# Cross-attention query panels without pieces between them, the norm root ahead of a cast, and the decode softmax ahead of heads 1 to 3

## What is computed

```
def cross_attn(h, mk, mv, w_q, w_o):
    q = (h @ w_q).reshape(B, T, X_HEADS, X_HEAD_DIM)           # 4 heads of 128
    s = jnp.einsum('bthd,bmhd->bhtm', q, mk) * (X_HEAD_DIM ** -0.5)
    p = jax.nn.softmax(s, axis=-1)
    o = jnp.einsum('bhtm,bmhd->bthd', p, mv).reshape(B, T, X_DIM)
    return o @ w_o
xp = xp + cross_attn(rmsnorm(xp, g_cross), mk, mv, w_xq, w_xo)                    # 256 tokens, one memory of 256
xs = xs + cross_attn(rmsnorm(xs, g_cross), cache_mem_k, cache_mem_v, w_xq, w_xo)  # 8 tokens, a memory of 256 each
```

## Time and profile before

| what | value |
|---|---|
| median of 3 runs | 1651.37 us (1646.44 to 1657.36) |
| profiled execution | 1649.72 us, its span 1648.0 us |
| TensorE busy | 1521.5 us, 92% of the span |
| VectorE busy | 1031.0 us, 63% |
| ScalarE busy | 612.7 us, 37% |
| mean granted TensorE clock | 0.966 of full speed |
| query stage | 736.3 us (first xq pass) to 822.9 us (first xo pass) |

### The profile page before, as it was taken

The page is one execution under the profiler, slowest core; times in us unless marked ns, Lnnn a source line. Parts: engine busy times, 40 slices in busy tenths (PEclk is TensorE's granted clock), DMA queues, the critical chain, the costliest instruction groups (busy, mean ns, idle before and its releaser), DMA issues.

```text
span 1648.0 us, 32704 instructions
## 1 busy us (share of the span) xinstructions
PE 1521.5 (92%) x12249; PEld 1408.8 (85%) x12249; DVE 1031.0 (63%) x3226; ACT 612.7 (37%) x721; POOL 235.1 (14%) x331
## 2 busy tenths in 40 slices
PE   4999987799898899998789999999999999999997
PEld 4999864577776677998589999999999999999996
DVE  4579899998976876665365555554444555554444
ACT  3342232232233453443354333333333333333443
POOL 3011222222222222330140000000000000000221
PEclk9999989999998999997799999999999999999998
DMA  8558999999998799552335555544555555553553
GB/s 319 179 180 303 405 361 413 407 378 373 373 383 312 265 401 398 177 180 77 128 125 175 184 181 178 178 154 158 177 184 198 184 184 184 181 178 125 187 179 123
DMA packets 78980, 388.42 MB, mean 236 GB/s; under 512 B 9097, under 2 KB 9873, under 8 KB 56865
## 3 DMA queue, kind: packets, MB, share of 16 engines
q1 hardware_dynamic: 35424, 230.90, 39.1%
q0 software_dynamic: 39376, 143.15, 23.1%
q10 hardware_dynamic: 4080, 13.12, 2.0%
HBM read 377.03 MB, written 10.10 MB: 235 GB/s over the span
## 4 chain that ended last, share of the span: by engine, by line
PE 74%; DVE 14%; DMA 5%; ACT 4%; issue 3%; ACTq 0%; DVEq 0%; SPq 0%; POOLq 0%; POOL 0%
PE bank L1541 22%; PE bank L1542 21%; PE bank L1543 21%; DVE page L1082 4%; DVE wlo L1026 3%; DMA page<-kc_dram 2%; PE bank L1698 2%; ACT whi L601 1%; ACT whi L564 1%; DMA raw<-p_out_dram 1%; DVE wlo L991 1%; PE bank L1894 1%; DMA raw<-p_in_dram 1%; DMA page<-vc_dram 1%; DVE rstd L1017 1%
## 5 line engine op out<-in xcount | busy, mean ns | idle before, releaser
L1541 PE MATMUL bank<-hh,whi 128*128 128x264 f32 (+1 forms) x2368 | 696.3, 294 | 36.9 <-DVE wlo L1026 23.9
L1542 PE MATMUL bank<-hl,whi 128*128 128x264 f32 (+1 forms) x2368 | 678.5, 287 | 0.0
L1543 PE MATMUL bank<-hh,wlo 128*128 128x264 f32 (+1 forms) x2368 | 677.9, 286 | 0.0
L991 DVE TENSOR_TENSOR wlo<-raw,whi 128x2048 fp32r<-128x2048 f32 (+1 forms) x174 | 357.9, 2057 | 276.1 <-ACT whi L564 276.1
L1541 PEld LDWEIGHTS bank<-hh,whi 128*128 128x128 f32 x2368 | 454.5, 192 | 73.9 <-issue 41.7
L564 ACT ACTIVATE whi<-raw 128x2048 fp32r<-128x2048 f32 (+1 forms) x174 | 299.3, 1720 | 552.9 <-PE bank L1543 545.4
L1542 PEld LDWEIGHTS bank<-hl,whi 128*128 128x128 f32 x2368 | 454.8, 192 | 0.7 <-issue 0.2
L1543 PEld LDWEIGHTS bank<-hh,wlo 128*128 128x128 f32 x2368 | 452.2, 191 | 0.0
L1082 DVE CUSTOM_DVE_ANT_0 page<-page,qb 128x128 f32<-128x128 f32 x1024 | 226.2, 283 | 16.5 <-ACT qb L646 11.4
L1541 PE MATMUL bank<-f_hi,whi 128*128 128x264 f32 x704 | 201.9, 287 | 7.5 <-DVE f_lo L1513 7.5
L1543 PE MATMUL bank<-f_hi,wlo 128*128 128x264 f32 x704 | 201.4, 286 | 0.0
(11 more groups left out here) (296 smaller groups left out, 1434.9 us busy)
## 6 DMA issues: line engine op xcount, KB each, us to landing
raw<-p_gu_dram SPq DMA_DIRECT2D x88, 1024.0 KB, 4.9
page<-kc_dram POOLq DMA_DIRECT2D x128, 512.0 KB, 8.1
page<-vc_dram POOLq DMA_DIRECT2D x128, 512.0 KB, 8.4
raw<-p_in_dram SPq DMA_DIRECT2D x48, 1024.0 KB, 8.4
raw<-p_dn_dram SPq DMA_DIRECT2D x64, 704.0 KB, 4.1
raw<-p_out_dram SPq DMA_DIRECT2D x16, 1024.0 KB, 5.2
raw<-p_mem_dram SPq DMA_DIRECT2D x8, 1024.0 KB, 8.3
x_res<-x_fm_dram SPq DMA_DIRECT2D x8, 528.0 KB, 10.5
```

Source lines behind the costliest of these rows:

```text
L991: tt(wlo[:, (k + 2) % 4, 0:blocks * P], raw[:, (k + 2) % 4, 0:blocks * P], whi[:, k % 2, 0:blocks * P], ALU.subtract).then_inc(S("w_split" ...
L1541: mm(out, blk(whi, k % 2, b), rh, start=start, stop=False)
L1542: mm(out, blk(whi, k % 2, b), rl, start=False, stop=False)
L1543: return mm(out, blk(wlo, k, b), rh, start=False, stop=stop)
```

## The change

Nothing is added or taken away; instructions change places on three engines. On TensorE panels 0 and 1 run without any piece up to the last quarter of panel 1; a head's rows move from the first quarter of the next panel to its third, its spread from the second quarter of the next panel to the first quarter of the panel after that, and head 0's score, transposition and value product move back accordingly. On ScalarE the root stands ahead of the cast of panel 2. The decode softmax moves ahead of head 2's maximum on VectorE and ahead of head 2's exponential on ScalarE.

```
@@ -890,29 +890,29 @@
                 wait_apart(act, "a_ops", n + 1)
                 act.activation(oh[:, i:i + 1, 0:NP_], row(a_set(n)[-1][:, 0:256]), ACT.Copy).then_inc(S("a_ohi"), 1)
 
+            norm_root(2, T)
             step("xq", 0, 0, C)
-            norm_root(2, T)
             x_rows(0)
+            step("xq", 0, 1, C)
             x_stage(0)
-            step("xq", 0, 1, C)
+            x_rows(1)
             x_exp(H)
-            x_rows(1)
+            step("xq", 0, 2, C)
             x_scale(H)
-            step("xq", 0, 2, C)
-            x_pt(H)
             x_rows(2)
             step("xq", 0, 3, C)
+            x_pt(H)
+            x_rows(3)
             x_out_hi(H, 0)
-            x_rows(3)
             x_stage(1)
+            x_exp(H + 1)
             x_stage(2)
-            x_exp(H + 1)
+            x_scale(H + 1)
+            act.wait_ge(S("x_sub"), 1)
+            act.activation(x_p[:, :, :, 0:XH], x_s, ACT.Exp).then_inc(S("x_exp"), 1)
             x_exp(H + 2)
-            x_scale(H + 1)
             x_pt(H + 1)
             x_scale(H + 2)
-            act.wait_ge(S("x_sub"), 1)
-            act.activation(x_p[:, :, :, 0:XH], x_s, ACT.Exp).then_inc(S("x_exp"), 1)
             x_pt(H + 2)
             x_out_hi(H + 1, 1)
             x_take(0)
@@ -1420,14 +1420,14 @@
             x_start()
             ch.link(dve.memset(x_p, 0.0))
             step("xq", 0, 0, C, to_q)
+            step("xq", 0, 1, C, to_q)
             x_scores(0)
             x_max(H)
-            step("xq", 0, 1, C, to_q)
+            step("xq", 0, 2, C, to_q)
             x_rec(H)
             x_scores(1)
-            step("xq", 0, 2, C, to_q)
+            step("xq", 0, 3, C, to_q)
             x_scores(2)
-            step("xq", 0, 3, C, to_q)
             x_out_lo(H, 0)
             x_start()
             x_max(H + 1)
@@ -1436,18 +1436,18 @@
             bh = "p (b h) -> p b h"
             tt(x_sm[:, 0:32].rearrange(bh, b=ND), x_s[:, :, 0, :], x_s[:, :, 1, :], ALU.max).then_inc(S("x_small"), 1)
             x_rec(H + 1)
-            x_max(H + 2)
             dve.wait_ge(S("x_small_ps"), 1)
             ch.link(dve.tensor_reduce(x_sm[0:32, 64:65], bank[5][0:32, 0:P], AX.X, ALU.max))
             ts(x_sm[0:32, 96:128], ident[0:32, 0:32], x_sm[0:32, 64:65], None, ALU.mult).then_inc(S("x_small"), 1)
-            x_rec(H + 2)
             dve.wait_ge(S("x_small_ps"), 2)
             mb = bank[5][:, P:P + 32].rearrange(bh, b=ND)
             for m in range(2):
                 ins = tt(x_s[:, :, m, :], x_s[:, :, m, :], mb, ALU.subtract)
             ins.then_inc(S("x_sub"), 1)
+            x_max(H + 2)
             dve.wait_ge(S("x_exp"), 1)
             tt(x_sm[:, 32:64].rearrange(bh, b=ND), x_p[:, :, 0, 0:XH], x_p[:, :, 1, 0:XH], ALU.add).then_inc(S("x_small"), 1)
+            x_rec(H + 2)
             x_out_lo(H + 1, 1)
             x_start()
             dve.wait_ge(S("x_small_ps"), 3)
@@ -1940,20 +1940,19 @@
 
             for k in range(4):
                 x_quarter(k, 0)
+                if k >= 2:
+                    x_spread(k - 2)
+                x_quarter(k, 1)
+                if k == 2:
+                    x_head(0)
+                x_quarter(k, 2)
                 if k:
                     x_rows(k - 1)
-                x_quarter(k, 1)
-                if k:
-                    x_spread(k - 1)
-                x_quarter(k, 2)
-                if k == 1:
-                    x_head(0)
-                elif k == 2:
-                    x_turned(H)
-                elif k == 3:
-                    x_out(H)
                 x_quarter(k, 3)
+            x_turned(H)
+            x_spread(2)
             x_rows(3)
+            x_out(H)
             for k in range(2):
                 pe.wait_ge(S(f"acc{k}_free"), ACC["xq"] // 2 + 3)
             x_head(1)
@@ -1961,9 +1960,9 @@
             x_head(2)
             pe.wait_ge(S("x_small"), 1)
             pe.transpose(bank[5][0:32, 0:P], x_sm[:, 0:32], ident).then_inc(S("x_small_ps"), 1)
-            x_turned(H + 1)
             pe.wait_ge(S("x_small"), 2)
             mm(bank[5][:, P:P + 32], ones[0:32, :], x_sm[0:32, 96:128], start=True, stop=True).then_inc(S("x_small_ps"), 1)
+            x_turned(H + 1)
             x_turned(H + 2)
             x_out(H + 1)
             pe.wait_ge(S("x_small"), 3)
```

## The result

| | before | change |
|---|---|---|
| median beside each other on one chip | 1649.32 us (4 runs, 1646.44 to 1657.36) | 1633.05 us (4 runs, 1631.62 to 1637.91) |
| ratio | | 0.9902 [0.9873, 0.993] |
| profiled execution, span | 1649.72, 1648.0 us | 1634.03, 1632.3 us |
| mean granted clock | 0.966 | 0.970 |

The change is faster by 1.0%; the spans of the two profiled executions differ by 15.7 us. Of these 15.4 lie in the cross query stage: from the norm sum (L1593, which runs 0.34 us earlier than before) to the first output pass (L1541 with `oh`) the stage took 81.19 us before and 65.80 now.

A forecast was written before the change was run, and what follows sets the result against it. The stage was taken as bound by TensorE's in-order list, waits on pieces within it and the low clock. From 1649.72, -20.5 + 3.1 + 2.2 + 0.9 + 0.7 = -13.6 gives 1636.1, median-adjusted 1637.8, stated as 1637 us; range 1629 to 1645.

The forecast's parts named there:

- A: The panels, to panel 3's evacuation: 20.5 us shorter if nothing waits and the clock stays up.
- the margins of 1.6 and 0.8 us: TensorE asks for x_q[0] 1.6 us after it is ready, and for panel 2's split 0.8 us after.
- the removed wait: TensorE's 4.75 us wait for VectorE's x_q at the end of panel 0, which the change was to remove.
- The clock: Within the panels: a fall to 1.2 GHz after each of two spreads, 3.4 us each, costing +3.1 us, bounds 0 and 6.2.
- rival 1: The clock stays up in the panels and beyond: -19.1 us, 1630.6, or 1632 carried to the median; chance 0.18.
- B: End of panel 3 to the decode softmax: a chain of cast, split, scores, spread 3, scores; +2.2 us.
- C: Decode softmax to first value product, with the softmax moved ahead of head 2: +0.9 us, bounds 0 and +2.
- D: First value product to first output panel: same work, clock perhaps back later; +0.7 us, bounds 0 and 3.4.
- The case with the highest chance: Whole kernel: a time within 1% of before, neither below 1634.9 nor above 1667.9 us; chance 0.63.

The follow-up runs named there:

- wide spreads: Spreads multiply 128 zero-padded rows in place of 8: ratio 0.9872 on the change, 0.9946 on the kernel before, 0.9917 on that with the root ahead.
- VectorE's list cleared: The change with 128-row spreads, first value product ahead of head 2's transposition, output panels' splits later on VectorE: 0.9885, or 0.9876 with splits in two gaps.
- the repeat: The change itself, unaltered, timed once more beside the kernel before: ratio 0.9895.
- values first: The change with head 1's value product, the decode sums and the first value product ahead of head 2's transposition: ratio 0.9851.

## Why the prediction was right

**A.** The sum of passes, spreads, head and transpositions was right. It put the end of panel 3, at the full clock, 24.5 us behind the norm sum (2.86 to 744.55, and 21.6). In the change panel 3 ended 26.2 us behind it (767.57); without the 1.5 us of the one fall that is 24.7. VectorE was scoring head 1 and reached the evacuation 0.6 us later, at 768.16, which makes 26.81; the prediction had no such term. With wide spreads and no fall A was 25.05, and with VectorE's list cleared 23.90. No wait was left; the margins of 1.6 and 0.8 us held, the second as 1.0 (split done at 747.5, panel 2 from 748.5).

Where the 18.2 us come from the experiments tell, with 0.45 us lost for each low microsecond. Before, A without its 23.9 low microseconds would be 34.3 us (measured with one fall left: 35.12 - 1.5 = 33.6). The root ahead brings it to 30.1, the order of the panels to 25.05. So, all with wide spreads, 3.5 us are the root's (33.6 to 30.14), 5 us the order's, and 9 us (0.45 x the 20.5 low microseconds that went) the clock's; 0.4 us are assigned to none. The other runs agree: beside the repeat, the six runs of the change were on average 16.9 us shorter than the eleven of before and, by the mean granted clock of each, 19.8 us less at 1.2 GHz, which is 9 us. The prediction had the sum, but its text named the removed wait first; half of the gain was the clock.

**The clock.** The term was +3.1 us for two falls of 3.4 us; the profiled execution had one (+1.5), the repeat two. The mechanism was as read from the earlier trace rows: a fall with TensorE busy throughout, behind a spread. The rule of the Trainium skill that was weighed (TensorE: Matmul & The Clock Gate, section "HAM oscillation"), that pauses between bursts cost the clock, is borne out for the pause of 4.76 us, behind which the clock fell even with wide spreads; it does not cover the fall at 752.5, ahead of which the trace has no pause. Panels without a fall, as in rival 1, did occur: in the change with values first, whose panels are the same. How often the clock falls cannot be told from one trace, and the range had to hold both.

**B.** The chain of the prediction came out term by term: cast at 767.61, split at 769.55, scores, spread 3 at 775.32 with 3.75 us, scores, L1437 at 782.56. From the start of the cast it is 14.95 us, where 14.9 was summed. In the repeat A changed by -17.2 us, where -17.4 was forecast, and B by +2.3, where +2.2 was.

**C** was the term that was mis-sized: +0.9 forecast, -0.14 measured (0 was its lower bound). The prediction charged head 2's maximum 2 us for standing behind the decode maximum and gave only half of it back. In the trace both exchanges cancel, and with the softmax moved back C is 0.14 us longer: this part of the change is worth nothing that the runs can show.

**D** grew by 1.24 us, forecast 0.7, and by 0.05 us in the repeat: the term goes with the clock and differs from execution to execution. In the first one the first two value products and the scores of head 3 still ran at 1.2 GHz (1.08 and 0.99 us for the products, against 0.64), the clock returned some 5 us behind the first value product, and before within 1 us of it (granted clock 0.81 from 809 to 810 us, 1.00 from there).

The differences of all stretches make the forecast 2.1 us too slow in the trace. The median is 4 us under it: 1637 forecast, 1633.05 measured beside 1649.32, which is itself 2 us under the 1651.37 from which the prediction started. The case with the highest chance, a time within 1% of before, came true by very little: the ratio is 0.9902, and its interval reaches to both sides of 0.99. On which side it came to lie is luck.

## What to carry to other kernels

When a wait of one engine's list goes, sum the stage again at the full clock and price the clock apart: here half of the gain was 20 us at 1.2 GHz that went when the wait and the pieces between the passes did. A small matmul group among large passes may cost more afterwards than while it runs, so compare the clock behind it with a form that fills the array. And work that is moved into a gap has to be put there again each time something ahead of it moves.

## What the runs showed that was not expected

- A spread of 16 matmuls on 128 rows of zero-padded weights takes no longer than one on 8 rows, and the clock behaves otherwise behind it. Of the executions whose panels had no wait of 4.8 us, the clock fell within the panels in none of the five with wide spreads and in five of the seven with spreads on 8 rows. The wide spread is also 0.2 to 0.3 us shorter from its start to the next pass (1.70 to 1.81 against 1.97 to 1.98 us); no run separates that from the number of rows, and nothing was run on numbers of rows between 8 and 128.
- The same list loses the clock in one execution and not in another: 3.4 and 6.8 low microseconds in two executions of the change, 0.0 in a kernel with the same panels. By 0.45 us for each low microsecond, an estimate, about 3 us of the spread between runs of one kernel can come from this.
- The table load of the root runs ahead of the root's wait: at 739.31, 3.1 us before the root could start (742.44). Ahead of the cast it costs nothing; behind it, it stood on the path with 1.28 us.
